# A hybrid recurrent layer on one core: branch products woven into the third mixer, sums added by GpSimd, signals per pair of banks, a ring that runs on

## What is computed

```
h = x + 1/2 * SwiGLU_1(RMSNorm(x))            # 2048 -> 2*5504 -> 2048
u = RMSNorm(h);  P = u @ w_in
y_A = GatedDeltaNet(short conv + SiLU on q/k/v, per-head decay)
y_B = GLA(low-rank forget gate)
y_C = RWKV7(token shift, data-dependent decay)
m = sum_i sigmoid(P_gate_i) * (y_i @ w_branch[i])   # y_i 768 wide
h = h + m @ w_out
x = h + 1/2 * SwiGLU_2(RMSNorm(h));  final RMSNorm
def _head_rmsnorm(o, g):
    return o * lax.rsqrt(jnp.mean(o * o, axis=-1, keepdims=True) + NORM_EPS) * g
# GatedDeltaNet, per head and sample sequence:
S_t = exp(g_t) (I - beta_t k_t k_t^T) S_{t-1} + beta_t k_t v_t^T ; o_t = S_t^T q_t
# GLA:  S_t = diag(exp(gk_t)) S_{t-1} + k_t v_t^T ; o_t = S_t^T q_t
```

## Time and profile before

| | us |
|---|---|
| median of 3 executions | 3481.86 (3481.29 to 3482.83) |
| the profiled execution | 3482.45 |
| its span | 3480.7 |
| mean granted clock of PE, of full speed | 0.941 |

### The profile page before, as it was taken

One profiled execution on the slowest core, in us unless ns is written; L12 is line 12 of the kernel. 1 busy time (PEld: TensorE's weight loads), 2 busy tenths in 40 slices (PEclk: granted clock), 3 DMA queues, 4 the chain that ended last, 5 costly groups with the idle time before them and its releaser, 6 DMA issues.

```text
span 3480.7 us, 59713 instructions
## 1 busy us (share of the span) xinstructions
PE 3194.7 (92%) x23222; PEld 3066.8 (88%) x23222; DVE 1774.8 (51%) x2266; ACT 1180.0 (34%) x1550; POOL 68.8 (2%) x139
## 2 busy tenths in 40 slices
PE   6999999999799999999998997469999999999998
PEld 6999999999799899888897885449989999999997
DVE  4554345543446666556586544347545553355434
ACT  3333333333334422222254221226443333233332
POOL 2000000000000000001000001000000000000000
PEclk9999999999899999999999996559999999999999
DMA  4555445554355423234452332016646554455542
GB/s 137 163 162 163 155 143 163 163 164 154 103 161 157 126 91 96 85 97 117 157 177 87 90 111 81 31 51 213 189 121 169 165 161 149 153 167 161 159 153 88
DMA packets 596089, 472.51 MB, mean 136 GB/s; under 512 B 28872, under 2 KB 541280, under 8 KB 595598
## 3 DMA queue, kind: packets, MB, share of 16 engines
q1 hardware_dynamic: 578960, 435.53, 41.9%
q0 software_dynamic: 6288, 21.47, 2.2%
q10 hardware_dynamic: 10704, 13.61, 1.1%
HBM read 447.10 MB, written 23.38 MB: 135 GB/s over the span
## 4 chain that ended last, share of the span: by engine, by line
PE 81%; DVE 11%; ACT 4%; issue 2%; DMA 1%; POOL 0%; DVEq 0%; ACTq 0%; POOLq 0%
PE ps L350 23%; PE ps L351 22%; PE ps L352 22%; DVE lo L653 2%; PE ps L996 1%; PE ps L986 1%; PE ps L486 1%; ACT hi L495 1%; PE ps L2094 1%; DVE cvA L1869 0%; DVE xl L833 0%; PE ps L991 0%; PE ps L1763 0%; PE ps L1254 0%; PE ps L1772 0%
## 5 line engine op out<-in xcount | busy, mean ns | idle before, releaser
L350 PE MATMUL ps<-xh,hi 128*128 128x288 f32 x4800 | 1455.9, 303 | 77.1 <-ACT kept L562 21.6
L351 PE MATMUL ps<-xl,hi 128*128 128x288 f32 x4800 | 1433.3, 299 | 0.0
L352 PE MATMUL ps<-xh,lo 128*128 128x288 f32 x4800 | 1431.2, 298 | 0.0
L653 DVE TENSOR_TENSOR lo<-raw,hi 128x1024 fp32r<-128x1024 f32 x820 | 982.3, 1223 | 603.5 <-ACT hi L495 593.2
L495 ACT ACTIVATE hi<-raw 128x1024 fp32r<-128x1024 f32 x820 | 839.8, 1053 | 918.0 <-PE ps L352 870.8
L350 PEld LDWEIGHTS ps<-xh,hi 128*128 128x128 f32 x4800 | 917.8, 191 | 105.6 <-issue 36.4
L351 PEld LDWEIGHTS ps<-xl,hi 128*128 128x128 f32 x4800 | 919.3, 192 | 0.5
L352 PEld LDWEIGHTS ps<-xh,lo 128*128 128x128 f32 x4800 | 918.8, 191 | 0.0
L350 PE MATMUL ps<-hidh,hi 128*128 128x288 f32 x1376 | 413.0, 300 | 26.5 <-DVE x L693 14.8
L351 PE MATMUL ps<-hidl,hi 128*128 128x288 f32 x1376 | 411.9, 299 | 0.0
L352 PE MATMUL ps<-hidh,lo 128*128 128x288 f32 x1376 | 409.6, 298 | 0.0
(11 more groups left out here) (679 smaller groups left out, 2295.5 us busy)
## 6 DMA issues: line engine op xcount, KB each, us to landing
raw<-in_w_ff_up SPq DMA_DIRECT2D x688, 256.0 KB, 4.2
raw<-in_w_in SPq DMA_DIRECT2D x448, 256.0 KB, 3.0
raw<-in_w_ff_down SPq DMA_DIRECT2D x344, 256.0 KB, 3.3
raw<-in_w_out SPq DMA_DIRECT2D x64, 256.0 KB, 3.2
raw<-in_w_branch SPq DMA_DIRECT2D x48, 256.0 KB, 3.1
gatesD<-kept ACTq DMA_DIRECT2D x24, 288.0 KB, 2.6
gates<-gatesD SPq DMA_DIRECT2D x8, 864.0 KB, 7.2
raw<-in_w_branch SPq DMA_DIRECT2D x48, 128.0 KB, 3.4
```

Of the source, the lines that this page charges most:

```text
L350: pe.matmul(out, w, rh, start=start, stop=False)
L351: pe.matmul(out, w, rl, start=False, stop=False)
L352: return pe.matmul(out, wl, rh, start=False, stop=stop)
L653: dve.tensor_tensor(lo[:, q, :], raw[:, q, :], hi[:, q, :].bitcast(F32), SUB).then_inc(lo_ready[q], 1)
```

## The change

1. **Down phases.** The two bodies of 22 (21) slots become one straight run of 44 (42). PE waits for the hidden tiles one by one (`hid_lo`), goes through the pairs of banks in the order 2, 3, 0, 1 (2, 3, 1, 0 in the second half), and after the last slot of each of the first three pairs signals `pair_ready`; DVE waits for these and drains a pair while PE works on the next. PE's wait for empty banks at the entry of down phases and of the up phases behind them is gone.
2. **Ring.** The place is `(slot0 + s) % RING`, counted through all phases.
3. **Branches.** Two of three branches (`brC`, `brA`, 32 of 48 slots) are woven work now, behind `gate` (212 slots in all); their products are stored through `kept` in `rawsD`. In the branch phase, 16 slots, DVE multiplies branch B alone; ACT issues the loads of gates and of the stored products (`load_gates`, `load_raws`, two pairs ahead); GpSimd multiplies the stored products by their gates and adds the two into `merged`; DVE adds the third. y of C and of A is split at the head of mixer B.
4. **Norms.** ACT takes Ln from PSUM, with scale and epsilon in the instruction (`act_root_of`); DVE's `fin_eps` steps are gone (six executions).
5. **Sample heads of A.** The first product of head h+1 stands before the update of head h, with three state buffers; the mask is put on the keys (`kdm`) rather than on the result.
6. **Table U.** shift 60 to 40, conv 4 to 3, bfeat 6 to 9, bgk 20 to 22, bfin 10 to 16, bprod 3 to 4, bsco 1 to 2, bsso 4 to 5; `aszt` is gone. The wait for stored sample states of B moves behind B's head norm.

```diff
-            add(f"down{f}{h}", tiles, 2, 4)
+            add(f"down{f}{h}", 2 * tiles, 1, 8)
...
-    add("branch", 12, 4, 6)
+    add("brC", 8, 2, 4)
+    add("brA", 8, 2, 4)
+    add("branch", 8, 2, 4)
...
-WOVEN = ("inA", "inB", "inBt", "gate")
+WOVEN = ("inA", "inB", "inBt", "gate", "brC", "brA")
...
+        def ring(p, s):
+            return (p["slot0"] + s) % RING
...
# PE, down phases
+                            turn, k = divmod(s, HALVES[h])
+                            pe.wait_ge(hid_lo, f * FT + h * HALVES[0] + k + 1)
+                            for pos, pair in enumerate(down_pairs(h)):
+                                if k == 0:
+                                    pe.wait_ge(acc_empty, turn * 4 + (p["group0"] + pos - 3))
...
+                                if k == HALVES[h] - 1 and pos < 3:
+                                    mm.then_inc(pair_ready, 1)
...
# DVE, branch phase
-                            if n == 0:
-                                dve.tensor_tensor(merged[:, bass.ds(m, 2), :], gg, br,
-                                                  MUL).then_inc(acc_empty, 1)
...
+                            dve.wait_ge(gate_ready, it * 4 + (FT + g + 1))
+                            dve.tensor_tensor(gated[:, :, :], gg, ps[:, g % 2 * 2:g % 2 * 2 + 2, 0:NT],
+                                              MUL).then_inc(acc_empty, 1)
+                            dve.wait_ge(acc_empty, G + 1)
+                            dve.wait_ge(sem("raws_summed"), 2 * it * 4 + 2 * (g + 1))
+                            mm = merged[:, bass.ds(m, 2), :]
+                            dve.tensor_tensor(mm, mm, gated[:, :, :], ADD).then_inc(sem("gated"), 1)
...
# GpSimd, behind the sample states of mixer B
+            for pair in range(KD // 2):
+                pool.wait_ge(gate_ready, FT + pair + 1)
+                pool.wait_ge(sem(f"raws_landed{pair % 2}"), 16 * (pair // 2 + 1))
+                r2 = raws[:, pair % 2, :, :]
+                pool.tensor_tensor(r2, r2, gates[:, pair % 2, 0:3:2, :], MUL).then_inc(sem("raws_summed"), 1)
+                pool.wait_ge(sem("raws_summed"), 2 * pair + 1)
+                pool.tensor_tensor(merged[:, 2 * pair:2 * pair + 2, :].rearrange("p c t -> p (c t)"),
+                                   r2[:, 0, :], r2[:, 1, :], ADD).then_inc(sem("raws_summed"), 1)
...
+        def act_root_of(e, act, sq_, scale, k, sums):
+            e.need("hn_sum", sums)
+            e.mark(act.activation(sq_[:, :, :], ps[:, 0:6, 0:NT], ACT.Ln, scale=scale, bias=epsilons[:, k:k + 1]), "sums_read")
...
# DVE, sample heads of mixer A (PE's side has deltas(h + 1) ahead in the same way)
+                    masked(0)
+                    deltas_out(0)
                     for h in range(6):
...
+                        e.mark(dve.tensor_tensor(t["z"][0:32, h, :], ps[0:32, 5, 0:P], t["zb"][0:32, h, :], ADD), "ss_z_kept")
+                        if h < 5:
+                            deltas_out(h + 1)
+                        weave(U["assz"])
```

More of the change, by code:

```diff
@@ L86, in plan @@
     add("gate", 8, 12, 2)
-    add("branch", 12, 4, 6)
+    add("brC", 8, 2, 4)
+    add("brA", 8, 2, 4)
+    add("branch", 8, 2, 4)
     add("out", 8, 4, 2)
     ff(1)
-    use, group = [0] * RING, 2
+    slot, group = 0, 2
     for p in ph:
-        p["base"] = list(use)
-        p["per"] = [len(range(q, p["n"], RING)) for q in range(RING)]
-        p["group0"] = group
-        use = [u + p["times"] * c for u, c in zip(use, p["per"])]
+        assert p["times"] == 1 or p["n"] % RING == 0
+        p["slot0"], p["group0"] = slot, group
+        slot += p["times"] * p["n"]
         group += p["times"] * p["groups"]
@@ L498, in phase @@
                 p = PLAN[name]
-                size = {"up": 4, "do": p["n"], "br": 2}.get(name[0:2], 4)
+                size = {"up": 4, "do": p["n"] // 2, "br": 2}.get(name[0:2], 4)
                 def body(it):
                     for s in range(p["n"]):
-                        q = s % RING
-                        if not (name == LAST and it == 1 and s + AHEAD >= p["n"]):
+                        q = ring(p, s)
+                        if not (name == LAST and s + AHEAD >= p["n"]):
                             split(ahead(p, s, it))
+                        if name == "branch" and s % 2 == 0:
+                            act.wait_ge(sem(f"gates_landed{s // 2 % 2}"), it * 32 + 16 * (s // 4 + 1))
+                            gg = gates[:, s // 2 % 2, :, :]
+                            act.activation(gg, gg, ACT.Sigmoid).then_inc(gate_ready, 1)
                         if (s + 1) % size:
@@ L1343, in act_mixC @@
             weave.presplit(2)
[L1344 to L1346 removed]
+            act.wait_ge(sem("consts"), 2)
+            act_root_of(e, act, sqC, 1.0, 0, 1)
             weave(U["kk"])
@@ L1804, in act_mixA @@
                 weave.presplit(2)
-                e.need("fin_eps")
-                e.link(act.activation(sqA[:, :, :], sqA[:, :, :], ACT.Ln))
-                e.mark(act.activation(sqA[:, :, :], sqA[:, :, :], ACT.Exp, scale=-0.5), "fin_rs")
+                act_root_of(e, act, sqA, 1.0, 0, 1 if half else 3)
                 weave(U["head"])
@@ L1977, in dve_mixA @@
+                        weave(U["asso"])
             weave(U["afin"])
@@ L2156, in act_mixB, with split_y, rest_y @@
             weave(U["bfin"])
[L2157 removed]
             e.link(act.activation(proj[:, 12:18, 0:NT], proj[:, 12:18, 0:NT], ACT.Silu))
[L2160 to L2161 removed]
+            act.wait_ge(sem("gates_free"), 1)
+            act.wait_ge(sem("kept_stored"), 16 * (GROUPS_A + GROUPS_B + GROUPS_G))
+            for pair in range(2):
+                load_gates(act, pair)
+            act_root_of(e, act, sqB, 1.0 / P, 0, 1)
             weave(U["bfin"])
             act.wait_ge(sem("B_whole"), 1)
[L2164 to L2170 removed]
+            for pair in range(2):
+                load_raws(act, pair)
+            split_y(act, 2 * BT, 3 * BT)
+        def split_y(act, k0, k1):
+            for y in Y_ORDER[k0:k1]:
+                act.activation(y_high(y), ybuf[:, y, :], ACT.Copy).then_inc(sem("y_hi"), 1)
+        def rest_y(dve, k0, k1):
+            for k in range(k0, k1):
+                y = Y_ORDER[k]
+                dve.wait_ge(sem("y_hi"), k + 1)
+                dve.tensor_tensor(y_low(y), ybuf[:, y, :], y_high(y).bitcast(F32), SUB).then_inc(sem("y_ready"), 1)
         def dve_mixB(dve, weave):
```

331 lines of the change are left out of this document (171 added, 160 removed).

## The result

The changed kernel takes 3432.97 us (median of 4, 3422.91 to 3435.32) against 3482.35 us before (4 runs): a ratio of 0.9853, 95% interval 0.9833 to 0.9873. It is faster, by 49 us; 166 were forecast, and the range ended at 3370. Its profiled execution took 3434.02 us, with a span of 3432.0 us.

What follows compares the result with a forecast made beforehand. PE, busy 3194.7 of 3480.7 us, was taken as the bound, with its idle time and slow clock to be won. 3482.45 - 60 - 23.5 - 83 = 3315.95, forecast as 3315 us; range 3280 to 3370.

Steps and rivals of the forecast that it cites:

- Part 1: Feed-forward down phases and ring: PE's waits for drains and hidden tiles go, -60 us, bounds -50 and -66.
- Part 2: Early mixers: less woven work in shift and conv, and shorter roots, -23.5 us, bounds -12 and -30.
- Shift: Shift stage of the early mixers: 20 woven units less, gain near the splits' time, -7.5 us.
- Conv: Mixer A's conv: 18 woven units less, DVE sets the end, -8 us, bounds -5.5 and -14.3.
- The roots: Norm roots, six executions: DVE's 1.96 us step between PE's sums and ACT's Ln goes, -8 us, bounds -4 and -11.8.
- the woven work that is taken out here isn't gone: Early mixers: slots taken out move back into the late idle stretch and cover idle time, counted in Part 3.
- Part 3: A's sample heads to the branch phase's end: 374 us become 291, -83, bounds -105 and -55.
- about 13.4 warm: Mixer B's prompt blocks: each block's own PE work, 26.7 us cold, takes about 13.4 at full clock.
- rival 1: Late mixer stages: splits of woven slots lengthen the ACT and DVE chain, gain 55 rather than 83, 3343 us; chance 0.2.
- 7 each, bound by the loads: Branch phase: each of 8 pairs takes 7 us, set by 6.9 us of loads, 56 in all.
- Rival 2: Branch phase: GpSimd and DVE exclude each other, phase up to 68 us, +12, 3327 us; chance 0.12.
- Rival 4: Branch phase: GpSimd bounds it, deciding from 7 us a pair; kernel slower than before, above 3489 us; chance 0.03.

Runs made afterwards that it cites:

- e1: Kernel before with only the feed-forward change (straight down phases, a signal per bank pair, single hidden-tile waits, running ring): 3420.39 us, ratio 0.9828.
- e2: Changed kernel with 4 woven units more at kk and 4 less at fin2, restoring the old group places in mixer C: 3407.61 us, ratio 0.9787.
- e6: Changed kernel with 4 rather than 2 woven units between chunks of mixer B's prompt blocks, 16 less at bfin: 3423.55 us, one execution.
- e7: Changed kernel with 5 rather than 2 woven units behind each sample head of mixer A, taken from afin and afin2: 3415.3 us, one execution.
- e8: Changed kernel with mixer C's old places, the sigmoid a pair ahead and slots split ahead of A's and B's head norms: 3386.62 us, ratio 0.9727.
- e4: Changed kernel with two slots split ahead of the roots of the head norms of A and B: 3409.81 us, ratio 0.9799.
- e3: Changed kernel with ACT's sigmoid of the next pair's gates ahead of its wait for this pair's sum: 3419.32 us, ratio 0.9822.
- e9: Kernel of e3 with the product and addition of the stored sums on DVE instead of GpSimd: 3417.29 us, one execution.
- e13: Kernel of e8 with the product and addition of the stored sums on DVE instead of GpSimd: 3384.1 us, ratio 0.9712.
- e5: Changed kernel with no woven units between chunks of mixer B's prompt blocks (2 in the changed kernel): 3423.38 us, one execution.
- e12: Kernel of e8 with no woven units in mixer B, all run behind it, first gate and sum loads after them: 3426.78 us, one execution.

## Why the prediction was wrong

**Part 1 was right.** Forecast -60; the two stages with the feed-forwards give -65 in the changed kernel's trace and -66 in e1's, and e1's median, against its own runs of the kernel before, gives -60. PE's waits for `x` and `hidl` are gone, which the prediction named as the sign, and the windows are full at clock 1.00. The other sign, over 0.95 of clock in all but one or two slices, did not come.

**Part 2: the direct terms were about half right, and a term of another kind was missing.** Shift gave 4.6 for 7.5. Conv gave 1.2 in the changed kernel's profile and 4 in that of e2, for 8; kernels with the same code there took 68.5 to 71.6 us, so its gain is 1 to 4, below the lower bound of 5.5. The roots gave about what was forecast: from PE's last sum to DVE's next multiplication the chain is 2.0 us shorter in C's last norm and in each half of A (5.14 for 7.14 and 7.15), and 0.7 in the first of C, 6.7 for 8. (C's last stage is 5.8 us shorter in the table: a wait of PE for `kept` behind the root, 4.8 us in the kernel before, is gone there too.) The missing term is e2's: the step "the woven work that is taken out here isn't gone" followed the matmuls, but not the places at which a group ends. ACT's copy of a group moved by 4 units through every stage behind, and came to stand ahead of splits and masks: 14 us in C's solves and 2 in the stage ahead of them. C's stage with its sample heads is 5 us longer, of which e2 brought back one, and the stage of A ahead of its sample heads is 3; for the rest no run shows a cause. The whole part was +11 rather than -23.5.

**Part 3 failed, by 92 us, half of it at the clock.** This is the step that took the forecast out of its range. The stages against the forecast: heads of A 75 for 56, norm 26 for 18, entry 36 for 35.5, blocks and sample heads of B 129 for 100.5, end of the weave 40 for 25, branch phase 77 for 56. The two misses of 19 and 28 us are stretches in which PE has hardly a gap and a clock of 0.63 to 0.78; the two norms make 23 and the branch phase 21. The sum took their woven matmuls at 0.1325 us and put the small ones at "about 13.4 warm", since it tied the half clock to the idle time. The rows had shown both together; the changed kernel parts them, with PE busy for 25.00 of 25.00 us at a clock of 0.51. Filling the idle time is not enough there; e6 and e7 raised the clock only with still more of wide work, to 0.73 and 0.81. That the clock sets the time of such a stretch is seen where the code is the same: the six heads of A took 64.0 us at a clock of 0.57, 59.7 at 0.63 (e2) and 56.5 at 0.67 (e8). The prediction named a clock that stays down in its last sentence, as what would make it wrong at its root, and gave it neither a price nor a chance. The price could be had from the rows: at half clock the blocks are 53.5 for the small matmuls and 50 for the woven ones at most, 103 for 61, and the heads stay at 75 for 56, so 3376 already, beyond the range's 3370. (The blocks came to 76 us, since their clock was 0.65 and not 0.5 throughout.)

The norms missed by 8 and 15 us, mostly through splits queued behind the roots (e4 took 16 of them back, and left a wait of 6.1 us for `kept` in the second). This was in the text as rival 1, with the right engines, but as a cost to the chain; what paid was PE, in its woven work.

The branch phase missed by 21 us. The step that failed is "7 each, bound by the loads": the prediction set 4.8, 4.5, 4.7 and 6.9 us beside each other and took the largest, where the order of ACT put the sigmoid's 1.6, GpSimd's 4.9 and DVE's and ACT's steps behind one another, 9.95 us a pair. Of the 21 us, e3 took back 7 by that order and e9 2.6 more by leaving GpSimd out; the cause of the other 12 stays open.

**Rival 2 was true in its mechanism** and small: DVE's steps with two inputs in SBUF stand still while GpSimd's product runs. The Trainium skill (SBUF — State Buffer, Who interferes with whom) says that a DVE instruction with two inputs in SBUF contends with a GpSimd instruction that reads SBUF. The trace agrees, with 3.07 and 2.84 us against 0.76 and 1.23. Its price was put at 12 us of the phase; e9 gave 2.6, since other things bounded the pair as well. **Rival 4** would have needed more than 7 us of GpSimd a pair: it takes 4.9 (2.65 and 2.28), a little over the rows' 4.5, and part of that is time in which DVE held it up (see the last section).

**Where the changed kernel lies behind e1.** Their profiled executions are 20 us apart in the stages of the table: C's solves +15, its sample heads +6, the stage ahead of them +4, A up to its heads +4, the tail +9, the last stage +2; against them shift -5, C's last norms -6, A's roots -4, conv and the first stages -3. What e2, e3 and e4 repair are orders of instructions, not the idea of the change: e8 and e13 have all parts of the change (e13 but for GpSimd's sums) and are 34 and 36 us faster than e1, and 46 and 49 faster than the changed kernel.

## What to carry to other kernels

An engine that is full is not an engine at speed: before idle time is filled, ask what the granted clock will be with the work that is then there, price both levels, and put the doubled time into the range. When work is moved through a list of places, follow not only the work but what is tied to its count (copies, stores, signals at the end of a group): with groups of 16, a shift by 4 cost more than the 20 units brought. And per-engine sums bound a loop only from below; write down the cycle through all engines in their program order, and look for the step that stands behind a wait and needs nothing of it.

## What the runs showed of the hardware

- GpSimd's elementwise step was 2.65 us for a product of 1152 columns of fp32. DVE does it in 1.36, and an addition of 576 columns in 0.76. Where GpSimd's product had begun first, DVE's steps with two inputs in SBUF hardly advanced: `xl` (0.76 alone) ended 0.6 us behind its end and `lo` (1.23 alone) 1.1, whenever they had started. It holds the other way too: GpSimd's addition of 576 columns took 2.28 us where DVE's split still ran for the first 1.0 of it, and 1.79 where `xl` still ran for the first 0.54; so some 1.25 us undisturbed, by an estimate from the two. DVE's product of `gates` and PSUM kept its 0.74 beside GpSimd's additions in the changed kernel, and beside a product in e3.
- The clock stayed at 1.2 GHz (0.51 in the mean) in a stretch of 25 us in which PE had no gap, with nine wide matmuls for 36 small ones; with 18 it went up and down between the two levels (mean 0.73).
- The same instructions got different clocks in different executions: the sample heads of mixer A, with the same code in ten of the kernels, took 56.5 to 59.7 us in the profiles of six and 62.4 to 64.0 in those of four, at clocks of 0.63 to 0.68 and 0.57 to 0.59. The sample heads of mixer C took 133.0 to 139.3 us in seven kernels with the same code, at clocks of 0.88 to 0.84. The first alone is 0.2% of the kernel, and the executions of one kernel here lay 2 to 19 us apart; e5, e6, e7, e9 and e12, with one execution each, are read by their stages for this reason, not by their totals.
